# One core, two transformer blocks in 32-bit floats: the same tiles in another order of addresses

## The reference

```
for l in range(2):
    h = rmsnorm(x, mix_norm_g[l])
    x = x + token_mixers(h, ...)          # h @ w_in, four mixers (retention, SSD, GLA, mLSTM),
                                          # merged = sum(gates * (y_n @ w_branch[n])), merged @ w_out
    h = rmsnorm(x, ffn_norm_g[l])
    if l % 2 == 0:
        x = x + (silu(h @ w1) * (h @ w3)) @ w2            # dense, 2816 wide
    else:
        x = x + moe_ffn(h, ...)           # 8 experts, the best 2 of each token, each 2816 wide
x = rmsnorm(x, final_norm_g)
```

## The kernel before

| tile | address before | mod 64 | address after | mod 64 |
|---|---|---|---|---|
| ring | 16512 | 0 | 16512 | 0 |
| x, low_rows, hT, hT_hi | 50304 to 83071 | 0 | 104704 to 137471 | 0 |
| w_hi, w_lo | 83072, 99456 | 0 | 196384, 212768 | 32 |
| merged, gates, u_z, xs, scratch, cst | from 115840 | 0 | from 137472 | 0 |
| gain, small, table and others | from 160992 | as listed in the code | from 182624 | the same |
| third_gu | 174752 | 32 | 50304 | 0 |
| down_w | 191136 | 32 | 66688 | 0 |
| fhT_hi, fhT_lo | 215712, 217760 | 32 | 91264, 93312 | 0 |
| xg_lo | 219808 | 32 | 95360 | 0 |
| u_ret, ch_in, conv, probs, y, yT (mixers) | from 174752 | 32 | from 50304 | 0 |
| u_ml (mixers) | 187072 | 0 | 62624 | 32 |

## Time and profile before

### The profile page before, as it was taken

One profiled execution on the slowest core, in us unless ns is written; L12 is line 12 of the kernel. 1 busy time (PEld: TensorE's weight loads), 2 busy tenths in 40 slices (PEclk: granted clock), 3 DMA queues, 4 the chain that ended last, 5 costly groups with the idle time before them and its releaser, 6 DMA issues.

```text
span 2819.0 us, 30806 instructions
## 1 busy us (share of the span) xinstructions
PE 2530.2 (90%) x11371; PEld 2000.4 (71%) x11371; DVE 1644.3 (58%) x2283; ACT 1319.0 (47%) x1687; POOL 404.7 (14%) x224
## 2 busy tenths in 40 slices
PE   6998789989987799999999999969987997997997
PEld 5885568878755577777777777748666885775786
DVE  2456555524565488888888888843435544243554
ACT  1332134413431277777777777723424442442443
POOL 2344100003541000000000000024510002540000
PEclk9999899999997899999999999979999998999999
DMA  5423075424231399998998998843346533345550
GB/s 187 162 95 143 35 246 187 135 98 142 103 142 48 114 367 307 326 346 304 326 346 305 325 347 305 279 140 125 130 165 225 185 114 113 134 163 185 174 192 30
DMA packets 373374, 549.30 MB, mean 195 GB/s; under 512 B 20948, under 2 KB 273224, under 8 KB 373144
## 3 DMA queue, kind: packets, MB, share of 16 engines
q1 hardware_dynamic: 369072, 535.82, 55.7%
q0 software_dynamic: 3776, 9.80, 1.3%
q10 hardware_dynamic: 432, 2.37, 0.2%
HBM read 546.91 MB, written 1.05 MB: 194 GB/s over the span
## 4 chain that ended last, share of the span: by engine, by line
PE 61%; DVE 9%; DMA 3%; ACT 3%; issue 2%; POOL 1%; SPq 0%; ACTq 0%; DVEq 0%
PE mb L840 12%; PE mb L842 11%; PE mb L841 11%; PE pb L840 4%; PE pb L842 4%; PE pb L841 4%; PE pb L818 3%; PE pb L1164 3%; PE pb L823 2%; DMA ring<-in_w_in 2%; POOL w_lo L712 1%; DVE w_lo L2199 1%; ACT w_hi L1430 1%; PE pb L888 1%; PE mb L1118 1%
## 5 line engine op out<-in xcount | busy, mean ns | idle before, releaser
L2199 DVE TENSOR_TENSOR w_lo<-ring,w_hi 128x1024 fp32r<-128x1024 f32 x384 | 461.6, 1223 | 182.6 <-ACT w_hi L1430 132.0
L840 PE MATMUL mb<-w_hi,hT_hi 128*128 128x512 f32 x1232 | 498.9, 405 | 23.8 <-DVE xg_lo L2199 9.3
L842 PE MATMUL mb<-w_lo,hT_hi 128*128 128x512 f32 x1232 | 485.3, 394 | 0.0
L712 POOL TENSOR_TENSOR w_lo<-ring,w_hi 128x1024 fp32r<-128x1024 f32 x152 | 368.5, 2449 | 586.8 <-ACT w_hi L1430 586.3
L1430 ACT ACTIVATE w_hi<-ring 128x1024 fp32r<-128x1024 f32 x280 | 285.7, 1054 | 322.9 <-DMA ring<-in_w_in 191.8
L2199 DVE TENSOR_TENSOR w_lo<-down_w,w_hi 128x1024 fp32r<-128x1024 f32 x242 | 295.2, 1223 | 93.6 <-ACT w_hi L1430 79.3
L840 PE MATMUL pb<-w_hi,hT_hi 128*128 128x512 f32 x736 | 302.0, 410 | 17.0 <-DVE low_rows L2199 7.6
L841 PE MATMUL pb<-w_hi,low_rows 128*128 128x512 f32 x736 | 292.9, 398 | 0.0
L842 PE MATMUL pb<-w_lo,hT_hi 128*128 128x512 f32 x736 | 292.8, 398 | 0.0
L840 PEld LDWEIGHTS mb<-w_hi,hT_hi 128*128 128x128 f32 x1232 | 232.6, 189 | 79.9 <-issue 20.4
L1563 ACT ACTIVATE w_hi<-ring 128x1024 fp32r<-128x1024 f32 x256 | 268.1, 1056 | 42.5 <-PE mb L842 39.2
(11 more groups left out here) (412 smaller groups left out, 3807.6 us busy)
## 6 DMA issues: line engine op xcount, KB each, us to landing
ring<-in_moe_w SPq DMA_DIRECT2D x128, 1024.0 KB, 7.8
ring<-in_w_in SPq DMA_DIRECT2D x48, 2048.0 KB, 7.8
down_w<-in_moe_w SPq DMA_DIRECT2D x88, 1024.0 KB, 10.5
third_gu<-in_moe_w SPq DMA_DIRECT2D x48, 1024.0 KB, 8.7
down_w<-in_w_ffn_down SPq DMA_DIRECT2D x22, 1024.0 KB, 10.0
ring<-in_w_out SPq DMA_DIRECT2D x8, 2048.0 KB, 8.5
ring<-in_ffn_w SPq DMA_DIRECT2D x16, 1024.0 KB, 8.0
ring<-in_w_ffn_gate SPq DMA_DIRECT2D x16, 1024.0 KB, 5.4
```

The source lines that it names most:

```text
L712: nc.gpsimd.tensor_tensor(w_lo[:, m % NPIECE], source[m][0], w_hi[:, m % NPIECE].bitcast(F32), ALU.subtract).then_inc(pool_split, 1)
L840: mm(o, a_hi, hi, start=start, stop=False)
L842: return mm(o, a_hi, lo, start=False, stop=stop)
L2199: return tt(dst, src, hi.bitcast(F32), ALU.subtract)
```

## The change

The declarations of SBUF tiles are put in another order. `ring` stays first. Behind it come the mixers' buffers, with the dense stages' slots, `fhT_hi`, `fhT_lo` and `xg_lo` in the same memory (as before, at the same distances), and a filler tile up to the mixers' end. `w_hi` and `w_lo` come last. No instruction, wait, semaphore or size is changed.

```diff
         ring = sb("ring", [P, 2, SLOTW])
+        with ExitStack() as mixers_memory:
+            mixed = []
+
+            def mix(name, shape, dt=F32):
+                mixed.append(math.prod(shape[1:]))
+                return mixers_memory.enter_context(nc.sbuf_tensor(name, shape, dt))
+
+            u_ret = mix("u_ret", [P, T, 1024])
...
+            yT = mix("yT", [P, 2, 2, S])
+        third_gu = sb("third_gu", [P, GU_W])
+        down_w = sb("down_w", [P, NSLOT, DN_W])
+        fhT_hi = sb("fhT_hi", [P, 2, S], F32R)
+        fhT_lo = sb("fhT_lo", [P, 2, S], F32R)
+        xg_lo = sb("xg_lo", [P, KD, P], F32R)
+        sb("rest_of_mixers", [P, sum(mixed) - GU_W - NSLOT * DN_W - 4 * S - KD * P])
         x = sb("x", [P, T, D])
...
         hT_hi = sb("hT_hi", [P, KD, S], F32R)
-        w_hi = sb("w_hi", [P, NPIECE, PIECE], F32R)
-        w_lo = sb("w_lo", [P, NPIECE, PIECE], F32R)
         merged = sb("merged", [P, T, D])
...
         table = sb("table", [1, MAXPASS + 1], I32)
 
-        with ExitStack() as mixers_memory:
...
-        third_gu = sb("third_gu", [P, GU_W])
-        down_w = sb("down_w", [P, NSLOT, DN_W])
-        fhT_hi = sb("fhT_hi", [P, 2, S], F32R)
-        fhT_lo = sb("fhT_lo", [P, 2, S], F32R)
-        xg_lo = sb("xg_lo", [P, KD, P], F32R)
+        w_hi = sb("w_hi", [P, NPIECE, PIECE], F32R)
+        w_lo = sb("w_lo", [P, NPIECE, PIECE], F32R)
```

More of the change, by code:

```diff
@@ L10 @@
+import math
 import numpy as np
@@ L260, in build @@
         ring = sb("ring", [P, 2, SLOTW])
+        with ExitStack() as mixers_memory:
[4 more added lines that the diff above has]
+            u_ret = mix("u_ret", [P, T, 1024])
+            u_gla = mix("u_gla", [P, T, 4 + 2 * MW])
+            u_ml = mix("u_ml", [P, T, ML_O + MW + 8])
+            ch_in = mix("ch_in", [P, 13, S])
+            conv = mix("conv", [P, 10, S])
+            probs = mix("probs", [P, NH, 384])
+            xdt = mix("xdt", [P, T, MW])
+            y = mix("y", [P, T, MW])
+            yT = mix("yT", [P, 2, 2, S])
[5 more added lines that the diff above has]
+        sb("rest_of_mixers", [P, sum(mixed) - GU_W - NSLOT * DN_W - 4 * S - KD * P])
         x = sb("x", [P, T, D])
```

## The result

| | median | range | runs |
|---|---|---|---|
| before | 2817.43 us | 2813.73 to 2818.04 | 5 |
| after | 2836.79 us | 2829.96 to 2838.67 | 5 |

The changed kernel is slower by a ratio of 1.0065 (95% interval 1.0049 to 1.0081), which is 19.4 us between the medians. The forecast was 2833.7 us. The profiled execution of after took 2831.98 us, with a span of 2830.2 us. That span is 11.2 us longer than the one before.

A forecast was written before the change was run, and what follows sets the result against it. The prediction took the pace of successive split products on TensorE as the bound. Dense first products 9.3 us plus mixers 7.0 us gave +16.3 us: 2837.1 us against the profiled execution, 2833.7 us against the median, range 2793 to 2842.

The forecast's parts named there:

- Parts (1) and (2): Moving third_gu, down_w and mixers' buffers, and w_hi and w_lo as write targets, changes no durations: 0 us.
- Two of the signs: Profile after: VectorE, ScalarE, transfers change at most 10 ns an instruction; a steady 240 ns interval would mean a step on top.
- part (3): Split products: moving operands, now 32 bytes off a 64-byte line, keep or bring the slow pace, 6.7 ns a product.
- The last sentence of that argument: Split products with equal operand offsets are fast today, unequal ones slow; after the change every pair is unequal.
- The dense layers' first product: 1584 products, 0.875 of them at the fast pace, each lose 6.7 ns: 9.3 us, all on the chain.
- Experts: The experts' 3168 split products are at 233.3 ns already and stay there: 0 us.
- The mixers' 7.0 us: Mixers: 1300 split products on the chain, 80% at the fast pace, each lose 6.7 ns: 7.0 us.
- The sum of 16.3 us: Whole kernel: dense layers' first product plus mixers lose 16.3 us, 0.6% slower; chance 0.44.
- Only the stationary side counts: Rival: aligned stationary operands bring all split products to 226.5 ns, gaining 22 us, 2795.5 us; chance 0.30.
- The 1 us that the prediction let VectorE take: Deduction from the faster rival's 23.0 us gain, for VectorE becoming late in the experts: 1 us.
- A step on top: Rival: off-line moving operands cost 13.4 ns or far-end memory is slow; 62 us slower in all, 2879 us; chance 0.10.
- Nothing happens: Rival: the two pace levels come from something the change leaves alone, or only 16-byte lines matter; 2817.4 us; chance 0.16.

The follow-up runs named there:

- e3: Changed order with 32 bytes of filler ahead of ring and 32 more ahead of w_hi, all split-product operands 32 bytes off a 64-byte line: 2828.01 us, ratio 1.0035.
- e1: Changed order with 32 bytes of filler ahead of w_hi, so all split-product operands start on a 64-byte line: 2826.11 us, ratio 1.0032.
- e2: Order of before with 32 bytes of filler ahead of the mixers' buffers, putting fhT_hi, fhT_lo and xg_lo on a 64-byte line: 2814.07 us, ratio 0.9993.
- e5: Order of before with 480 bytes of filler ahead of fhT_hi, all split-product distances 0: 2792.37 us, ratio 0.9917.
- e8: Changed order with ea moved into small and 384 bytes of filler ahead of fhT_hi, all distances 0 modulo 256: 2797.63 us, ratio 0.9929.
- e9: e5 with 32 bytes of filler ahead of xg_lo, so it alone is at another distance: 2803.78 us, ratio 0.9948.
- e11: The same kernel as e5, run again beside e12: 2791.3 us, ratio 0.9901.
- e12: The same kernel as e8, run again beside e11: 2795.97 us, ratio 0.9925.
- e6: Order of before with 128 bytes of filler ahead of w_hi, everything behind moving along: 2834.18 us, one run.
- e7: Order of before with 192 bytes of filler ahead of w_hi, everything behind moving along: 2836.67 us, one run.
- e10: w_hi and w_lo shifted 16 bytes inside one joint tile, with filler ahead of fhT_hi, putting dense-layer operands at distance 16: 2819.35 us, one run.
- e4: Changed order with 32 bytes of filler ahead of w_hi and 32 more ahead of w_lo, which alone is off a 64-byte line: 2831.58 us, ratio 1.0047.

## Why the prediction came out as it did

**The bound was read rightly.** TensorE's pace was what moved the time. Parts (1) and (2) were taken at nothing, and nothing they were: `w_lo` from `ring` 1223 ns before and after, ScalarE's `w_hi` from `ring` 1056 and 1056, a load into `third_gu` 8.7 and 8.7 us. Two of the signs were badly chosen. Some short VectorE instructions of the mixers changed by far more than 10 ns, as they do between two executions of one kernel; and single intervals of 240 ns stand in the trace of before already, in the experts' first product, so they couldn't have told a step on top.

**The step that failed is the cause in part (3).** It reads "an off-line read on either side breaks the rhythm as it does now". The 64-byte line has no part in it: e3 has everything off a line and e1 nothing, and both run at 228.9 ns in the dense layers' first product and at 233.2 in their second. What showed in its place is the distance between the two operands modulo 256: 226.7 ns at 0 and 228.9 to 234.2 at the others tried. The rows of before could not tell this, because in them off line and at distance 224 were one and the same. The last sentence of that argument was the sound one, that pairs with equal offsets are fast and those with unequal ones slow; it holds modulo 256 and not modulo 64. That sentence alone would have given the same forecast. So the forecast came right in its number by luck in its main term: distance 32 happens to cost 6.6 ns, as 224 does; 64 would have cost 2.2 ns.

**The terms of the sum.** The dense layers' first product was put at 9.3 us, "some 3 us" a stage. Measured are +2.3, +3.2 and +5.1 us, and 9.4 us in all without the stretches at half clock. For a stage without such a stretch on either side (189.7 to 192.9) the working gives 528 x 0.875 x 6.6 ns = 3.0 us for the first product and 264 x 0.8 ns = 0.2 us for the second: the 3.2 measured. Experts: 0 predicted, +1.5 us measured, of which their second products' step from 233.6 to 234.3 ns gives 1056 x 0.7 ns = 0.7 us and the first's from 233.0 to 233.4 ns 2112 x 0.4 ns = 0.8 us. The mixers' 7.0 us can't be seen between the two profiled executions, whose mixers sum to 1389.6 and 1388.6 us, though the pace there did go from 226.9 to 233.3 ns. Seven profiled kernels with distance 0 there (before, e2, e5, e8, e9, e11, e12) sum to 1379.3 to 1389.6 us, mean 1384.3. The three at 32, 128 and 192 (after, e6, e7) sum to 1388.6 to 1395.9, mean 1392.5. That is 8.2 us more, with a spread in each set of about as much: it agrees with the 7.0 and doesn't prove it. The weakest part of the sum, the mixers' share of 7.0 us, is therefore unconfirmed. The sum of 16.3 us stands against 19.4 us between medians and 11.2 us between the profiled executions.

**The rivals.** "Only the stationary side counts" fell with the result, and with e2, where the stationary side alone came on a line and stayed slow. Its 22 us were well worked out for another case: with all operands at distance 0, e5 and e11 gained 24.4 and 25.7 us. Of that 16.4 us lie in the experts (the rival's 10.6 for their first product and 1056 x 6.7 ns = 7.1 for their second make 17.7) and 1.6 in each dense stage without a stretch of low clock (264 x 6.7 ns = 1.8). The 1 us that the prediction let VectorE take can't be told from nothing: in the experts, what TensorE lost in intervals of over 260 ns between its split products was 46.3 us before and 45.9 in e5, but 48.4 in e11, the same kernel as e5. "A step on top" fell too: the steady pace of after is 233.3 to 234.3 ns, and the far end of memory is fast in e5 (`fhT_hi` at 216192) and e8 (`w_hi` at 196352). "Nothing happens" fell with the result. The prediction tied it to the lines of 16 bytes of the Trainium skill, page "SBUF — State Buffer", section "Specifications (TRN2)"; e10 sets the operands one whole such line apart and is at 231.8 in place of 226.7 ns, so in this kernel a shift by a whole line isn't free.

**What the cause rests on.** Shown is that the distance modulo 256 sets the pace of groups with one distance, in both orders of memory; the fillers change nothing but addresses. Distances 0 and 192 were had in both orders, 224 in that of before alone and 160 in the changed one alone. Why the distance counts is only argued. The timeline of after, with TensorE's weight loads (PEld):

```profile
2203.23 0.39 PE L847 MATMUL mb<-w_hi,low_rows 128*128 128x512 f32 x1
2203.23 0.19 PEld L848 LDWEIGHTS mb<-w_lo,hT_hi 128*128 128x128 f32 x1
```

The load of the next product's stationary operand begins with the product before it and lasts 0.19 us of its 0.23. So the two run at once, and e9 has its longest interval where the load of the one operand at another distance runs. A relation between the addresses could matter through parts of the memory that both reads want at the same moment. That is a guess: no run here looks inside it, and the uneven prices (64 cheaper than 16) aren't explained by it. No experiment was made for products in full float32, but the others moved their operands: those of `ring` and `yT` (addresses worked out from the declared shapes) are at distance 96 in before, 128 in after, 160 in e7 and 224 in e6, and the median between their starts is 429 ns in all four. A distance of 0 is not among them.

## What to carry to other kernels

Where float32r products stream back to back with a weight load each and TensorE's pace is the limit, work out the addresses of both operands modulo 256 and make them equal for every pair that meets, with filler if need be: here 480 bytes gave 0.8 to 1.0%. A change that only moves tiles has to be read by such relations between addresses, not by each tile's own alignment, and when two levels of a pace are seen, ask what else differs between the two groups of operands before one property is named. One operand of a group left at another distance can cost as much as if all were (233.0 ns in e9). And a sign that is to tell two causes apart has to be looked for in the trace of before first: if it stands there already, it tells nothing.

## What the runs showed of the hardware that was not expected

- TensorE's pace in float32r products (128x512, a new stationary operand each) depends on the distance of the moving from the stationary operand modulo 256 bytes, between 226.7 and 234.2 ns where all have the same distance, and not evenly: 16 bytes cost 5 ns, 64 bytes 2.2 ns, 128 bytes 5.7 ns.
- One pair in three at another distance can bring the mean of the three to that of all at this distance (e9: 233.0 ns at 0, 224 and 0, made of 238.9, 228.5 and 232.5), or most of the way (e2: 231.4 ns at 0, 192 and 0). Other mixtures were faster than either member alone (e4 in the dense layers: 230.8 ns at 192, 192 and 224) or slower (e7, the experts' first product: 234.7 ns at 192, 224 and 192).
- Products in full float32 start 429 ns apart at distances of 96, 128, 160 and 224 alike (`ring` and `yT` in before, after, e7 and e6).
- Runs of one kernel differ by up to 28 us (e3: 2807.09 to 2835.39). The fastest had a mean granted clock of 0.960 and the slowest one of 0.949, so stretches at half clock are part of it, and a difference of a few us in a single execution tells little.
